# Forget attention of a two-block transformer on one core: heads transposed and scored in pairs, forget sums added as a broadcast row

## The chip, the cores and the metric

The kernel runs on one core of a Trainium2 chip, in float32 throughout. The metric is the device time of one execution in microseconds (us).

## What is computed

The reference is a chain of two transformer blocks on 512 tokens of 1024 features: a first block (gated delta rule, spatial gating, mixture of experts), and a second block with two layers, each an attention followed by a mixture of experts. The change is in the attention of the second block's first layer, the "forget attention" (`fox` in the names). It has 16 heads of 64 features:

```
proj = h @ w_in                                # 1024 -> 3 * 1024 + 16
q, k = rmsnorm(q, q_norm), rmsnorm(k, k_norm)  # per head, 64 features
log_f = log_sigmoid(f_logit + b_f)             # one number per token and head
cum = cumsum(log_f, over tokens)
s = q @ k.T * 64 ** -0.5 + cum[query] - cum[key]
p = softmax(where(key <= query, s, -inf))
o = (p @ v) @ w_out
```

`cum[query]` is one constant for a row of the softmax and cancels in it, so only `-cum[key]` has to be added to the scores. The attention of the second layer (`mla`, 96 features a head, no forget term) uses the same function of the kernel and is not changed.

## The kernel before

The kernel is a sequence of stages. A stage is a block in which each engine has its own list of instructions; all engines meet at its end. Within a stage they wait for each other by step numbers: `PE.done(ins, name)` counts a step of TensorE, `PE.wait(engine, name)` lets another engine wait for it (AC is ScalarE, DV VectorE, PO GpSimd, sp SyncE, the engine that only issues DMAs). Every engine works strictly in the order of its list. Tokens are in 4 blocks of 128 (T = 4, P = 128), and weights stream through a ring of four buffers in chunks of up to 2 MB, which `W.issue(sp)` loads on SyncE's queue as soon as the buffer's last reader is done.

**The projection stage** (L2331 to L2539) makes q, k and v in 24 jobs of 16 matmul passes with 512 columns. Beside them it makes the forget numbers: `forget` at job 8, `running_sums` at job 12, and ScalarE's copy of the negated sums (L2465). These go into the 65th column of every key head (`qkv_f[1][..., FD]`), while GpSimd writes 1.0 into the 65th column of every query head (L2533). A contraction over 65 features then gives score minus the key's sum, with no further instruction. VectorE also reduces 48 slabs of another weight matrix (`ada`) that are loaded by SyncE throughout the stage; the last thing that SyncE does in the stage is to issue the second 2 MB chunk of the output projection's weights (`fox_w_out`), whose buffer comes free with the last job.

**The attention stage** (`attention`, L2140 to L2308, called at L2541) walks over 64 units. A unit is a head and a block of 128 queries; block t needs (t + 1) x 128 keys. Units go by pairs of heads: (head 0, block 0), (head 1, block 0), (head 0, block 1), and so on, 8 units a pair. For each unit

- TensorE multiplies q and k (`S`, L2224) into one of three PSUM banks,
- VectorE adds the causal mask and takes the negated maximum in one instruction (`neg`, L2281), the mask being one tile for all heads, made once by GpSimd (L2300, L2302),
- ScalarE takes the exponential and its sum (`exp`, L2253), VectorE the reciprocal (`inv`, L2289),
- GpSimd multiplies by it (`share`, L2307),
- TensorE transposes the shares (`turn`, L2214), four units after their scores,
- ScalarE, or for the widest block VectorE, copies them out of PSUM (`pT`, L2263, L2296),
- and after both heads' units TensorE multiplies with v (`pv`, L2234). The two heads of a pair write to the lower and the upper 64 partitions of one bank, so each uses half of the array's columns.

q and k lie as tokens x features and are transposed by TensorE one head at a time (`turn_head`, L2191), 4 transposes each for q and for k, two pairs ahead in a ring of four heads, with copies by ScalarE (L2242) and VectorE (L2269). SyncE has nothing to do in this stage.

## Time and profile before

| | us |
|---|---|
| median of 3 runs | 2099.71 (2099.28 to 2102.07) |
| the profiled execution, its own time | 2096.7 |
| its span in the profile | 2095.0 |
| the projection stage | about 1049 to 1233.5 |
| the forget attention | about 1235.0 to 1329.5 |
| the other attention, for comparison | about 1715 to 1812 |

```text
span 2095.0 us, 20480 instructions
## 1 busy us (share of the span) xinstructions
PE 2017.3 (96%) x7494; PEld 1087.0 (52%) x7494; DVE 977.2 (47%) x1817; ACT 451.0 (22%) x1094; POOL 337.5 (16%) x474
## 2 busy tenths in 40 slices
PE   8999999999999999999899999999998999999994
PEld 4444444579884444444445457554444557544442
DVE  2444535557773024333454656343344467444333
ACT  1112111023342001100241136220004446320000
POOL 1000000000102000334200013103331003203333
PEclk9999999999999999999999999999999999999997
DMA  5223365610012234599816850047995120046996
GB/s 183 90 101 130 109 249 186 215 66 2 1 50 92 79 102 160 219 405 400 301 62 216 312 192 2 14 168 304 403 391 183 63 103 2 3 161 226 372 375 243
DMA packets 123511, 363.32 MB, mean 173 GB/s; under 512 B 27596, under 2 KB 33000, under 8 KB 110864
## 3 DMA queue, kind: packets, MB, share of 16 engines
q1 hardware_dynamic: 77856, 174.13, 23.4%
q10 hardware_dynamic: 30432, 157.30, 19.2%
q0 software_dynamic: 15120, 30.53, 4.2%
q8 instruction: 63, 1.03, 0.2%
q14 instruction: 40, 0.33, 0.0%
HBM read 335.60 MB, written 43.52 MB: 181 GB/s over the span
## 5 line engine op out<-in xcount | busy, mean ns | idle before, releaser
L1617 PE MATMUL bank<-ring,work 128*128 128x512 f32 x768 | 342.5, 599 | 3.3 <-DVE work L1633 3.3
L1617 PEld LDWEIGHTS bank<-ring,work 128*128 128x128 f32 x768 | 144.1, 193 | 167.8 <-issue 167.8
L1916 POOL DMA_INDIRECT work<-x_rows,small x168 | 169.1, 1007 | 269.5 <-DVE work L1881 197.4
L1628 PE MATMUL bank<-ring_halves,work 128*128 128x512 f32 x384 | 172.9, 593 | 4.0 <-DVE work L1642 4.0
L432 PE MATMUL bank<-featT,ring 128*128 128x512 f32 x384 | 170.3, 597 | 2.8 <-DMA ring<-in_w_in 2.8
L2404 PE MATMUL bank<-ring,featT 128*128 128x512 f32 x384 | 168.9, 601 | 1.6 <-DVE small L2493 1.6
L1345 PE MATMUL bank<-ring,work 128*128 128x512 f32 x384 | 166.5, 593 | 3.5 <-PEq L2186 2.4
L1639 DVE TENSOR_TENSOR work<-work,bank 128x256 f32<-128x256 f32 x48 | 20.2, 420 | 282.4 <-ACT work L1636 282.4
L2404 PEld LDWEIGHTS bank<-ring,featT 128*128 128x128 f32 x384 | 73.7, 193 | 93.8 <-issue 92.0
L1628 PEld LDWEIGHTS bank<-ring_halves,work 128*128 128x128 f32 x384 | 72.8, 190 | 95.0 <-issue 95.0
L1345 PEld LDWEIGHTS bank<-ring,work 128*128 128x128 f32 x384 | 72.3, 190 | 91.6 <-issue 91.6
L432 PEld LDWEIGHTS bank<-featT,ring 128*128 128x128 f32 x384 | 71.8, 192 | 84.7 <-issue 81.7
L531 PE MATMUL bank<-ring,featT 128*128 128x512 f32 x256 | 110.4, 593 | 0.9 <-PEq L412 0.9
L1636 ACT ACTIVATE work<-bank 128x256 f32<-128x256 f32 x48 | 18.4, 383 | 414.9 <-PE bank L1617 414.9
L2224 PE MATMUL bank<-work 65*128 65x384 f32 (+7 forms) x256 | 89.2, 434 | 0.5 <-DVE work L2269 0.5
L2307 POOL TENSOR_SCALAR ring_halves<-ring_halves,small 128x128 f32<-128x128 f32 (+3 forms) x128 | 67.7, 532 | 115.4 <-DVE small L2289 115.4
L1881 DVE STREAM_TRANSPOSE work<-work 128x1024 f32<-128x1024 f32 x42 | 85.0, 2024 | 0.0
L1062 PE MATMUL bank<-ring,featT 128*128 128x512 f32 x192 | 83.3, 593 | 1.0 <-PEq L811 1.0
L531 PEld LDWEIGHTS bank<-ring,featT 128*128 128x128 f32 x256 | 48.5, 190 | 61.4 <-issue 61.4
L2253 ACT ACTIVATE ring_halves<-bank,small 128x128 f32<-128x128 f32 (+3 forms) x128 | 67.5, 528 | 54.2 <-DVE small L2289 53.0
L286 DVE SCALAR_TENSOR_TENSOR ring_halves<-ring_halves,ismall 128x1024 f32<-128x1024 f32 x48 | 61.6, 1282 | 30.4 <-DMA ring_halves<-in_w_ada 26.8
L453 DVE TENSOR_SCALAR work<-bank,small 128x512 f32<-128x512 f32 x24 | 18.0, 751 | 107.4 <-PE bank L432 107.4
(444 smaller groups left out, 2826.7 us busy)
## 6 DMA issues: line engine op xcount, KB each, us to landing
ring<-in_w_in SPq DMA_DIRECT2D x15, 2048.0 KB, 12.5
ring<-in_moe_w_gate ACTq DMA_DIRECT2D x28, 1024.0 KB, 6.9
ring<-in_moe_w_up ACTq DMA_DIRECT2D x28, 1024.0 KB, 9.9
ring_halves<-in_moe_w_down ACTq DMA_DIRECT2D x28, 1024.0 KB, 10.2
ring_halves<-in_w_ada SPq DMA_DIRECT2D x48, 512.0 KB, 6.4
y_rows<-work ACTq DMA_DIRECT2D x48, 512.0 KB, 10.3
ring<-in_expert_w_gate ACTq DMA_DIRECT2D x14, 1024.0 KB, 7.9
ring<-in_expert_w_up ACTq DMA_DIRECT2D x14, 1024.0 KB, 10.9
```

The lines of the kernel that those rows point to most:

```text
L432: last = nc.tensor.matmul(bank[b % 4][:, :], w[:, k, (b % 4) * P:(b % 4 + 1) * P], featT[:, k, :], start=(k == 0), stop=(k == KD - 1))
L531: last = nc.tensor.matmul(uv_bank(j)[:, :], featT[:, k, t * P:(t + 1) * P], w[:, k, :], start=(k == 0), stop=(k == KD - 1))
L1062: last = nc.tensor.matmul(zg_bank(j)[:, :], featT[:, k, t * P:(t + 1) * P], w[:, k, :], start=(k == 0), stop=(k == KD - 1))
L1345: last = nc.tensor.matmul(bank[j % 4][:, :], outT[:, k, t * P:(t + 1) * P], w[:, k, :], start=(k == 0), stop=(k == KD - 1))
L1617: last = nc.tensor.matmul(gu_sum[par], xgT[par][:, k, :], w_gu[par][:, k, :, :], start=(k == 0), stop=(k == KD - 1))
L1628: last = nc.tensor.matmul(bank[5 + h][:, :], hT[par][:, k, :], w_dn[par][:, k, span(h)], start=(k == 0), stop=(k == KF - 1))
L1881: nc.vector.transpose(xgT[par].rearrange("p k (s b) -> p s k b", s=NQ), xg[par].rearrange("p (s a k) -> p s k a", s=NQ, k=KD)).then_inc(M_ ...
L1916: nc.gpsimd.indirect_dma_start(out=xg[par][:, s * QD:(s + 1) * QD], out_offset=None, in_=x_quarters, in_offset=bass.IndirectOffsetOnAxis(a ...
L2224: PE.done(nc.tensor.matmul(bank[i % N_S][:, 0:(t + 1) * P], qT[:, t * P:(t + 1) * P], kT[:, 0:(t + 1) * P], start=True, stop=True), ("S", i))
L2253: AC.done(nc.scalar.activation(sx[i % N_SX][:, 0:n], bank[i % N_S][:, 0:n], ACT.Exp, bias=mx[:, i:i + 1], scale=-1.0, accum_out=inv[:, i:i ...
L2307: PO.done(nc.gpsimd.tensor_scalar(x, x, inv[:, i:i + 1], 1.0, ALU.mult, ALU.mult), ("share", i))
L2404: last = nc.tensor.matmul(f_bank(j)[:, :], featT[:, k, t * P:(t + 1) * P], w[:, k, :], start=(k == 0), stop=(k == KD - 1))
```

## The change

It has four parts, all for the forget attention.

1. The 65th columns go. q and k have 64 features a head and are stored without a gap; the memset of ones falls away on GpSimd and VectorE.
2. The negated running sums (16 numbers a token) are transposed by TensorE at job 14 (`sums_by_row`), copied by ScalarE, and stored to DRAM by GpSimd's queue (`key_rows`, 16 heads x 512 keys). From there each head's row is loaded into all 128 partitions, once for each query block t with (t + 1) x 128 keys: 4 DMAs and 655 KB a head. Heads 0 and 1 are loaded on GpSimd's queue in the projection stage, heads 2 to 15 by SyncE in the attention stage, into four buffers in turn; head h >= 4 waits until VectorE has made the last `neg` of head h - 4. GpSimd then writes the causal mask into the diagonal 128 x 128 part of each tile with an `affine_select`, 4 for each head. VectorE's instruction adds this tile where it added the common mask.
3. q and k are transposed for two heads at once (`turn_pair`): 128 columns in, one head's features on the lower 64 partitions and the other's on the upper 64. The two heads' scores are then matmuls with a contraction over 64, one on each half of the array's rows.
4. The stage has a function of its own, `fox_attention`, with 32 steps of two units. A step's order on TensorE is q or k transposes of the next pair, `pv` of four steps back, both heads' `S`, both heads' `turn` of two steps back. Reciprocals are taken for two units at once; VectorE copies the upper head's transposed shares, ScalarE the lower head's and the output; scores have four banks and shares eight buffers.

```diff
         FD = DM // NHB
-        FW = FD + 1
-        QKV = T * NHB * FW
-        qkv_f = [work[:, i * QKV:i * QKV + T * NHB * n].rearrange("p (t h n) -> p t h n", t=T, h=NHB) for i, n in enumerate((FW, FW, FD))]
-        FOX_END = 2 * QKV + T * DM
+        qkv_f = [work[:, i * T * DM:(i + 1) * T * DM].rearrange("p (t h n) -> p t h n", t=T, h=NHB) for i in range(3)]
+        FOX_END = 3 * T * DM
...
-        gains = small[0:FD, 256:258]
+        gains = small[0:2 * FD, 256:258]
...
+        f_rows = work[0:NHB, F0 + 928:F0 + 928 + S]
+        key_rows = nc.dram_tensor("key_rows", [NHB, S], F32, kind="Internal").ap()
+        rows_stored, bias_landed, first_bias_landed = sem("key_rows_stored"), [sem(f"bias_landed{i}") for i in range(4)], [sem(f"first_bias_landed{i}") for i in range(2)]
+        B0 = FOX_END + 2 * 2 * S
+        SEG = [P * (t + 1) for t in range(T)]
+        bias_at = [[work[:, B0 + o:B0 + o + n] for o, n in zip((0, 128, 384, 768), SEG)],
+                   [work[:, o:o + n] for o, n in zip((F0, B0 + 1280, F0 + 128, B0 + 1536), SEG)],
+                   [work[:, F0 + 512 + o:F0 + 512 + o + n] for o, n in zip((0, 128, 384, 768), SEG)],
+                   [a[:, o:o + n] for a, o, n in zip((state, work, state, state), (0, F0 + 1792, 128, 512), SEG)]]
+
+        def load_bias(eng, h):
+            for t in range(T):
+                eng.dma_start(bias_at[h % 4][t], key_rows[h:h + 1, 0:SEG[t]].partition_broadcast(P)).then_inc(first_bias_landed[h] if h < 2 else bias_landed[h % 4], 16)
...
-        F_AT, CUM_AT, Q_AT, K_AT = 8, 12, 9, 17
+        F_AT, CUM_AT, ROWS_AT, Q_AT, K_AT = 8, 12, 14, 9, 17
...
+
+                def sums_by_row():
+                    AC.wait(pe, "cum")
+                    for t in range(T):
+                        last = nc.tensor.transpose(bank[0][0:NHB, t * P:(t + 1) * P], f_cum[:, t * NHB:(t + 1) * NHB], ident[:, :])
+                    PE.done(last, "cum_rows")
...
-                        AC.done(nc.scalar.activation(qkv_f[1][:, :, :, FD], T4(bank[0][:, NR:2 * NR], NHB), ACT.Copy, scale=-1.0), "cum")
+                        AC.done(nc.scalar.activation(f_cum, bank[0][:, NR:2 * NR], ACT.Copy, scale=-1.0), "cum")
+                    if j == ROWS_AT:
+                        PE.wait(act, "cum_rows")
+                        AC.done(nc.scalar.activation(f_rows, bank[0][0:NHB, :], ACT.Copy), "cum_rows")
                     if j in (Q_AT, K_AT):
                         i = 0 if j == Q_AT else 1
                         DV.wait(act, ("eps", i))
...
-                PE.wait(pool, ("sum",) + jobs[7])
-                PO.done(nc.gpsimd.memset(qkv_f[0][:, :, :, FD], 1.0), "ones_q")
+                AC.wait(pool, "cum_rows")
+                pool.dma_start(key_rows[:, :], f_rows).then_inc(rows_stored, 16)
+                pool.wait_ge(rows_stored, 16)
+                for h in range(2):
+                    load_bias(pool, h)
...
-        oT2 = attention(FW, *qkv_f, FOX_END, FOX_END + 2 * TURNED_HEADS * S, None, k_gain)
+        def fox_attention(q, k, v, turned_at, out_at):
...
+            sx = [halves_of_ring[:, i * BANK:(i + 1) * BANK] for i in range(8)]
...
+            NP = NHB // 2
+            both = range(2)
+            steps = [(p, t) for p in range(NP) for t in range(T)]
+            N = len(steps)
+            TURN_LAG, PV_LAG = 2, 4
+            END = N + PV_LAG
+            q_at = {T * (p - 1): p for p in range(1, NP)}
+            k_at = {T * (p - 1) + 2: p for p in range(1, NP)}
+            out_at_step = {T * p + T - 1 + PV_LAG: p for p in range(NP)}
+            select_at = {**{T * p - 1: 2 * p + 2 for p in range(1, NP - 1)}, **{T * p: 2 * p + 3 for p in range(NP - 1)}}
+            turn_bank, out_bank, X = (bank[4], bank[5]), bank[6], bank[7]
...
+            with nc.Block() as block:
+                @block.sync
+                def _(sp):
+                    for h in range(2, NHB):
+                        if h >= 4:
+                            DV.wait(sp, ("neg", 2 * (T * ((h - 4) // 2) + T - 1) + h % 2))
+                        load_bias(sp, h)
+                @block.tensor
+                def _(pe):
+                    def turn_pair(b, x, p, name):
+                        for t in range(T):
+                            last = nc.tensor.transpose(b[:, t * P:(t + 1) * P], x[:, t, 2 * p:2 * p + 2, :].rearrange("p h n -> p (h n)"), ident[:, :])
+                        PE.done(last, name)
+                    turn_pair(X, q, 0, ("q", 0))
+                    turn_pair(out_bank, k, 0, ("k", 0))
+                    for j in range(END):
+                        if j in q_at:
...
+                            turn_pair(X, q, q_at[j], ("q", q_at[j]))
+                        if j in k_at:
+                            AC.wait(pe, ("q", k_at[j]))
+                            turn_pair(X, k, k_at[j], ("k", k_at[j]))
+                        if j >= PV_LAG:
+                            i = j - PV_LAG
+                            p, t = steps[i]
+                            AC.wait(pe, ("pT", 2 * i))
+                            DV.wait(pe, ("pT", 2 * i + 1))
+                            if t == 0 and p:
+                                AC.wait(pe, ("out", p - 1))
+                            for s in range(t + 1):
+                                for m in both:
+                                    last = nc.tensor.matmul(out_bank[FD * m:FD * (m + 1), t * P:(t + 1) * P], v[:, s, 2 * p + m, :], pT[(2 * i + m) % len(pT)][:, s, :],
+                                                            start=(s == 0), stop=(s == t))
+                            PE.done(last, ("pv", i))
+                        if j < N:
+                            p, t = steps[j]
...
+                            if j >= 2:
+                                AC.wait(pe, ("exp", 2 * (j - 2) + 1))
+                            qT, kT = turned[p % 2]
+                            for m in both:
+                                PE.done(nc.tensor.matmul(bank[(2 * j + m) % 4][:, 0:(t + 1) * P], qT[FD * m:FD * (m + 1), t * P:(t + 1) * P], kT[FD * m:FD * (m + 1), 0:(t + 1) * P],
+                                                         start=True, stop=True), ("S", 2 * j + m))
+                        if TURN_LAG <= j < N + TURN_LAG:
+                            i = j - TURN_LAG
+                            for m in both:
+                                PO.wait(pe, ("share", 2 * i + m))
+                                if i:
+                                    (DV if m else AC).wait(pe, ("pT", 2 * (i - 1) + m))
+                                for s in range(steps[i][1] + 1):
+                                    last = nc.tensor.transpose(turn_bank[m][:, s * P:(s + 1) * P], sx[(2 * i + m) % len(sx)][:, s * P:(s + 1) * P], ident[:, :])
+                                PE.done(last, ("turn", 2 * i + m))
...
+                @block.scalar
...
+                    for j in range(END):
+                        if j in out_at_step:
+                            p = out_at_step[j]
+                            PE.wait(act, ("pv", T * p + T - 1))
+                            AC.done(nc.scalar.activation(outT[:, p, :], out_bank[:, :], ACT.Copy), ("out", p))
+                        if j < N:
+                            n = (steps[j][1] + 1) * P
+                            for m in both:
+                                i = 2 * j + m
+                                DV.wait(act, ("neg", i))
+                                if i >= len(sx):
+                                    PE.wait(act, ("turn", i - len(sx)))
+                                AC.done(nc.scalar.activation(sx[i % len(sx)][:, 0:n], bank[i % 4][:, 0:n], ACT.Exp, bias=mx[:, i:i + 1], scale=-1.0, accum_out=inv[:, i:i + 1]), ("exp", i))
...
+                        if TURN_LAG <= j < N + TURN_LAG:
+                            to, turned_x = keep_turned(act, 0, j - TURN_LAG)
+                            AC.done(nc.scalar.activation(to, turned_x, ACT.Copy), ("pT", 2 * (j - TURN_LAG)))
...
+                @block.vector
...
+                    for j in range(END):
+                        if j < N:
+                            p, t = steps[j]
+                            for m in both:
+                                i = 2 * j + m
+                                scores = bank[i % 4][:, 0:(t + 1) * P]
+                                PO.wait(dve, ("bias", 2 * p + m, t))
+                                PE.wait(dve, ("S", i))
+                                DV.done(nc.vector.tensor_tensor_reduce(scores, scores, bias_at[(2 * p + m) % 4][t], -1.0, 3.0e38, ALU.add, ALU.min, mx[:, i:i + 1]), ("neg", i))
+                        if TURN_LAG <= j < N + TURN_LAG:
+                            to, turned_x = keep_turned(dve, 1, j - TURN_LAG)
+                            DV.done(nc.vector.tensor_copy(to, turned_x), ("pT", 2 * (j - TURN_LAG) + 1))
+                        if j in k_at:
+                            keep_k(X, k_at[j])
+                        if j < N:
+                            AC.wait(dve, ("exp", 2 * j + 1))
+                            DV.done(nc.vector.reciprocal(inv[:, 2 * j:2 * j + 2], inv[:, 2 * j:2 * j + 2]), ("inv", j))
...
+                @block.gpsimd
+                def _(pool):
+                    def select(h, t):
+                        d = bias_at[h % 4][t][:, t * P:(t + 1) * P]
+                        if h < 2:
+                            pool.wait_ge(first_bias_landed[h], 16 * T)
+                        else:
+                            pool.wait_ge(bias_landed[h % 4], 16 * T * ((h - 2) // 4 + 1))
+                        PO.done(nc.gpsimd.affine_select(out=d, in_=d, compare_op=ALU.is_ge, fill=-3.0e38, base=0, pattern=[[-1, P]], channel_multiplier=1), ("bias", h, t))
+                    for h in range(3):
+                        for t in range(T):
+                            select(h, t)
+                    for j in range(N):
+                        for m in both:
+                            for i in both if j in select_at else ():
+                                select(select_at[j], 2 * m + i)
+                            x = sx[(2 * j + m) % len(sx)][:, 0:(steps[j][1] + 1) * P]
+                            DV.wait(pool, ("inv", j))
+                            PO.done(nc.gpsimd.tensor_scalar(x, x, inv[:, 2 * j + m:2 * j + m + 1], 1.0, ALU.mult, ALU.mult), ("share", 2 * j + m))
+            return outT
...
+        oT2 = fox_attention(*qkv_f, FOX_END, F0 - KD * S)
```

## Rows read from the trace of the kernel before

**Rows 1.** The page's busy line of TensorE: us, share, instructions.
```profile
PE 2017.3 (96%) x7494; PEld 1087.0 (52%) x7494; DVE 977.2 (47%) x1817; ACT 451.0 (22%) x1094; POOL 337.5 (16%) x474
```

**Rows 2.** Busy time of each engine in the steady part of the forget attention.
```profile
core 0: us, PE busy (x) PEld busy (x) DVE busy (x) ACT busy (x) POOL busy (x), PEclk, DMA share, GB/s
...
1240.00:1325.00 85.00, 85.00 (x656) 58.89 (x654) 57.71 (x217) 55.52 (x181) 32.10 (x61) 1.00 0.02 7
```

**Rows 3.** The first transpose of shares, in order of time.
```profile
1240.12 0.27 PE L2214 MATMUL bank<-ident,ring_halves 128*128 128x128 f32 x1
```

**Rows 4.** TensorE in order of time: start us, us, instructions (one pair).
```profile
1267.61 0.44 PE L2234 MATMUL bank<-featT,work 128*64 128x128 f32 x4
...
1275.48 1.10 PE L2234 MATMUL bank<-featT,work 128*64 128x128 f32 x16
1276.50 0.65 PE L2191 MATMUL bank<-ident,work 128*65 128x128 f32 x4
...
1277.21 1.02 PE L2224 MATMUL bank<-work 65*128 65x512 f32 x2
1278.07 0.38 PE L2214 MATMUL bank<-ident,ring_halves 128*128 128x128 f32 x2
1278.29 1.02 PE L2224 MATMUL bank<-work 65*128 65x512 f32 x2
1279.24 0.44 PE L2234 MATMUL bank<-featT,work 128*64 128x128 f32 x4
1279.61 0.65 PE L2191 MATMUL bank<-ident,work 128*65 128x128 f32 x4
1280.10 0.49 PE L2214 MATMUL bank<-ident,ring_halves 128*128 128x128 f32 x3
```

**Rows 5.** VectorE in order of time, one 512-key score block.
```profile
1278.27 0.70 DVE L2281 CUSTOM_DVE_ANT_0 bank<-bank,featT 128x512 f32<-128x512 f32 x1 [0.33 <-PE bank L2224]
1278.88 0.14 DVE L2281 DVE_READ_ACCUMULATOR2_ANT small<- 128x1 f32 x1
```

**Rows 6.** GpSimd's groups with shapes apart: busy us, mean ns.
```profile
L2307 POOL TENSOR_SCALAR ring_halves<-ring_halves,small 128x512 f32<-128x512 f32 x32 | 22.1, 692 | 20.4 <-DVE small L2289 20.4
...
L2307 POOL TENSOR_SCALAR ring_halves<-ring_halves,small 128x128 f32<-128x128 f32 x32 | 11.9, 372 | 24.8 <-DVE small L2289 24.8
...
L2302 POOL TENSOR_SCALAR_AFFINE_SELECT featT<-featT 128x128 f32<-128x128 f32 x2 | 0.6, 292 | 0.3 <-POOL featT L2300 0.2
```

**Rows 7.** SyncE's DMA issues in order of time, before the attention.
```profile
1207.60 0.33 SPq L262 DMA_DIRECT2D ring_halves<-in_w_ada  x1
1207.97 0.43 SPq L120 DMA_DIRECT2D ring<-in_fox_w_out  x1
...
1228.11 0.33 SPq L266 DMA_DIRECT2D ada_part<-ring_halves  x1
1234.10 0.38 SPq L120 DMA_DIRECT2D ring<-in_fox_w_out  x1
```

**Rows 8.** DMA issues of the whole run: KB each, us to landing.
```profile
ring<-in_moe_w_gate SPq DMA_DIRECT2D x4, 1024.0 KB, 4.8
...
x_rows<-work SPq DMA_DIRECT2D x8, 512.0 KB, 2.6
```

**Rows 9.** DMA from 1233 to 1250 us in 40 slices, and its issue.
```profile
GB/s 0 0 0 0 0 72 270 222 405 371 395 357 357 405 429 400 400 434 328 92 0 0 0 0 0 0 0 0 0 0 0 39 0 0 0 0 0 0 0 0
...
ring<-in_fox_w_out SPq DMA_DIRECT2D x1, 2048.0 KB, 7.8
```

**Rows 10.** TensorE in order of time after two pauses.
```profile
1027.10 5.39 PE L2024 MATMUL bank<-work,ones 128*128 128x512 f32 x12 [2.41 <-PEq L1324]
...
1046.17 1.94 PE L2049 MATMUL bank<-ident,work 128*128 128x128 f32 x8 [4.98 <-ACT work L2076]
```

**Rows 11.** Granted clock (PEclk) behind these two pauses.
```profile
1027.00:1031.00 4.00, 3.90 (x9) 1.82 (x10) 0.00 (x0) 3.92 (x5) 1.72 (x2) 1.00 0.48 136
1046.10:1049.40 3.30, 3.23 (x10) 2.10 (x10) 2.25 (x5) 1.50 (x4) 0.00 (x0) 0.50 0.00 0
```

More of the change, by code:

```diff
@@ L2366, in _ @@
             def _(sp):
-                load(sp, gains[:, 0:1], D["fox_q_norm_2"].rearrange("o p -> p o"))
-                load(sp, gains[:, 1:2], D["fox_k_norm_2"].rearrange("o p -> p o"))
+                for m in range(2):
+                    load(sp, gains[FD * m:FD * (m + 1), 0:1], D["fox_q_norm_2"].rearrange("o p -> p o"))
+                    load(sp, gains[FD * m:FD * (m + 1), 1:2], D["fox_k_norm_2"].rearrange("o p -> p o"))
                 cb_a.all_stored(sp)
```

65 lines of the change are left out of this document (57 added, 8 removed).

## Prediction

> **What bounds the kernel now.** I read the page's busy line first: TensorE is busy for 96% of the span [rows 1], so a change pays by what it takes from TensorE's path, and costs what it makes TensorE wait. Then the windows by stage: in 85 us of steady forget attention TensorE is busy for all 85, while VectorE and ScalarE are busy for 58 and 56, GpSimd for 32, and the DMA engines for 2% [rows 2]. The reader is to see an engine with no holes and three with slack. The timeline of TensorE gives the prices: a pair of heads takes 1279.24 - 1267.61 = 11.63 us [rows 4], and eight of them 93.0 us.
>
> The sum is made against the profiled execution's own time, 2096.7 us (span 2095.0 and 1.7 around it); the median of the runs shown is 2099.7, 3.0 above it, and I add that at the end. A measurement of this kernel can tell about 0.2%, 4.2 us, from no change.
>
> **Prices of TensorE.** Starts of successive groups [rows 4]: two 512-column passes take 0.86 us, so 128 columns take 0.107; two transposes take 0.22, also 0.11 each; the group of four head transposes takes 0.49. A `pv` group with 16 passes takes 1.02 us, where one after the other would be 1.71: its two column halves run beside each other. The group of 4 takes 0.37. Both fit (passes / 2 + 1) x 0.107 + 0.05: the halves overlap except for one pass, since each head makes two passes in a row, and 0.05 goes at the change of the array's shape. Entering `pv` costs another 0.09 to 0.10 (1278.29 + 0.86 = 1279.15 against 1279.24).
>
> **Part by part: a pair after the change, without waits.** Head transposes: 2 groups in place of 4, 0.97. Transposes of shares: 20, as before, 2.2. `pv`, as before: 2.77 for its four groups (0.37, 0.59, 0.80, 1.02; the middle two by the formula), and 0.40 to enter. Scores: per block of t + 1 key blocks four passes, which stood one behind the other (4.27 a pair). The row halves are not in the trace; the nearest row is `pv`'s column halves, so I take the same one-pass stagger, three passes of four, 3.21, and 4 x 0.08 for the third change of shape in each step. Bounds: two passes (2.14, full overlap) and four (4.27, none). Sum 0.97 + 2.2 + 2.77 + 0.40 + 3.21 + 0.32 = 9.87, 1.75 less than before. Other engines: VectorE loses one head copy and one reciprocal in two, ScalarE gains the output copy and loses a head copy; with 27 us of slack in 85 [rows 2] neither is the bound. Adding a bias tile costs VectorE nothing, as the mask was already read there [rows 5].
>
> **The loads of heads 4 to 15.** Here a wait takes the place of what is won. At step 3 of a pair (t = 3) VectorE ends the `neg` that frees head 4's buffer; call that moment 0. SyncE then issues four DMAs at a pitch of 0.37 us [rows 7], so the last starts at 1.1 and carries 262 KB. Its landing: a store of 512 KB lands after 2.6 us and a load of 1024 KB after 4.8 [rows 8]; at the 0.4 MB/us of [rows 9] the smaller size takes off 0.6 and 2.0, which leaves 2.0 to 2.8, and I take 2.5, nearer the load. So head 4 is there at 3.6 (3.1 to 3.9).
>
> GpSimd's list at that same step is: two `select` of head 4, share(6), two `select`, share(7). A share that is ready at about 2 us stands behind a mask for a head whose scores come five steps later. Four selects of 0.29 and two shares of 0.69 [rows 6] are 2.55; gaps between GpSimd instructions I take as 0.08 (0 to 0.15, the idle time before a select [rows 6]), 3.05 in all. TensorE needs share(6) and share(7) two steps later, for turn(3) in step 5, and everything is queued behind it there. Wanted at about 2.06 + 1.48 = 3.5 us (step 4, then `pv` and `S` of step 5), share(7) comes at 3.6 + 3.05 = 6.65.
>
> The loop closes: from there to the next such `neg` TensorE has turn(7) 0.43, head transposes 0.48, `pv` 0.90, `S` 1.04, a turn 0.22, `pv` 1.12, and the first 512-key score with its `neg`, 1.81 (score at 1277.21 to VectorE's last read at 1279.02 [rows 4, 5]): 6.00. With 0.1 for the hand-over a period is 3.6 + 3.05 + 0.1 + 6.0 = 12.75 us against 11.63: +1.12. This happens for heads 4, 6, ..., 14, six times. The odd head's loads and selects follow one step later, when GpSimd is already late, so they add nothing. Six bound pairs: +6.7. Two free ones: -3.5.
>
> **The start of the stage.** GpSimd's list begins with 12 selects, of which four wait for head 2; then, before share(0), two of head 3. Both heads are loaded by SyncE, whose last issue of the stage before is 2 MB of `fox_w_out` at 1234.10 [rows 7]. It lands at 1241.9, its bytes moving until about 1241.3 at 0.4 MB/us [rows 9]. Heads 2 and 3 stand behind it in the same queue: 1.31 MB more, 3.3 us, and 0.6 to the semaphore: 1245.2. Two selects (0.74) and share(0) (0.45), two more and share(1): 1247.6. TensorE reached its first turn at 1240.12 [rows 3] and would be there at about 1240.3 now (one more score pair, fewer head transposes). It waits 7.3 us.
>
> The Trainium skill ("DMA: Bandwidth & Descriptors", queue model) says that each DMA engine consumes a queue's descriptors in ring order. By it the landing is at 1245.2 as above; no row shows two such loads side by side.
>
> The pause has a second price. After a pause of 4.98 us [rows 10] the granted clock was 0.50, the lower level of 1.2 GHz, for 3.3 us; after one of 2.41 us it was 1.00, 2.4 GHz [rows 10, 11]. 3.3 us at half clock lose 1.65. Start: +8.95.
>
> **The rest.** Four transposes at job 14 stand on TensorE's path: +0.5. The 1.31 MB for heads 0 and 1 share the DMA engines with the slabs, 3.3 us of them; the last slab's store was issued at 1228.11 and the stage's last issue is at 1234.10 [rows 7], which with 2.6 us to land [rows 8] leaves 3.4 us, so nothing; without that cover up to 1 us. Selects of heads 0 and 1 (3 us) end before anything waits for them. The dropped memsets were off the path. Sum: 6.7 - 3.5 + 8.95 + 0.5 = +12.7: own time 2109.4, median **2112.4**.
>
> **Rivals.** (1) *Loads hidden, no slower than before.* If head 4's load landed before GpSimd came to it, the selects would fill its idle time and cost TensorE some 0.3 a pair: 8 x (10.2 - 11.63) = -11.4, with start and transposes -2.0: 2097.7. Place: share(6), share(7) of each pair. Price: 1 us of landing moves the whole by 6. The kernel breaks even at a period of 10.6, a landing 1.5 us after `neg`; four issues alone take 1.1 and no row lands in 0.4. Against it only that I may have misread who is queued behind whom. 12%.
> (2) *Row halves fully beside each other.* Scores take two passes: -1.07 in each free pair, -0.32 in each bound one (only t = 2 lies on the loop), -4.0 in all: 2108.4. For it, the two heads write different banks and partitions; against it the stagger of `pv`. 15%. The Trainium skill ("TensorE: Matmul & The Clock Gate", Part 3) has packed tiles start about 4 ns apart; this rule would give the two passes, though this case's `pv` rows show one pass more.
> (3) *No overlap of the halves*, so the change doesn't do what it says on TensorE: +4.0, 2116.4. 6%.
> (4) *The pauses inside the pairs cost clock too.* They would be about 1.8 and 0.9 us with a turn between them, shorter than the 2.41 that cost nothing. If each cost what the long one did, 6 x 1.65 = +9.9: 2122.3. A slower landing ends in the same place. 12%.
> (5) My forecast, 55%.
>
> If heads 2 and 3 don't queue behind the 2 MB, they land near 1241, the pause is 3.1 and keeps the clock: 5.8 less, a bound of the forecast and not a rival.
>
> **Numbers.** Bounds of the forecast: landing and gaps +-2.7 each, score passes +-4.0, start -5.8 and +1.9 (if a short packet takes as long as a long one, 5.2 us for two heads in place of 3.3). Not all fall one way: 2104 to 2120. To leave out no more than 2 in 10 with rivals on both sides the range is 2099 to 2124. Faster by over 0.2%: 0.08 (half of rival 1 and some tail), within 0.2%: 0.10, slower: 0.82.
>
> **What would show it.** In the profile after: a hole of TensorE of 6 to 7 us from about 1240, ended by GpSimd's share, with a clock of 0.50 behind it; GpSimd waiting for DMA into `work` or `state` at heads 2 and 3, then every 12 to 13 us; two short holes before `turn` in six pairs; and free pairs of 9.9 us at the end. A `S` group of two heads at t = 3 in 1.3 us says three passes, 0.9 two, 1.7 four. The forecast is wrong if `turn` never waits for GpSimd, if the first hole is under 3 us, or if the pairs in between are shorter than 11.6 us.

## The result, and the profile after

| | median us | runs | of the kernel before beside it |
|---|---|---|---|
| before | 2100.51 (2099.28 to 2102.07) | 4 | |
| after | 2157.06 (2149.86 to 2160.53) | 4 | ratio 1.0264, 95% interval 1.0237 to 1.0292 |

The change costs 56.6 us. The forecast was a cost of 12.7 us, with a range that ended at 2124. The profiled execution of after has a time of 2160.53 us and a span of 2158.7, 63.7 above the span of before; it is the slowest of the four, which is why the stages below are compared one by one.

The page of after, its busy line:

```profile
PE 2021.8 (94%) x7434; PEld 1085.2 (50%) x7434; DVE 967.8 (45%) x1784; ACT 447.7 (21%) x1079; POOL 359.2 (17%) x544
```

TensorE's busy time has hardly moved from [rows 1], so what was added is mostly waiting; what some stretches cost more at a lower clock was saved in others. TensorE in order of time, from the start of the attention stage (L2616 transposes heads, L2651 makes scores, L2660 transposes shares, L2639 multiplies with v, L1345 is the stage behind):

```profile
1239.53 2.89 PE L2616 MATMUL bank<-ident,work 128*128 128x128 f32 x12 [4.29 <-PEq L2375]
...
1254.57 0.48 PE L2660 MATMUL bank<-ident,ring_halves 128*128 128x128 f32 x1 [8.00 <-POOL ring_halves L2737]
...
1269.12 2.29 PE L2660 MATMUL bank<-ident,ring_halves 128*128 128x128 f32 x8 [5.86 <-POOL ring_halves L2737]
...
1280.44 0.85 PE L2660 MATMUL bank<-ident,ring_halves 128*128 128x128 f32 x6 [0.98 <-ACT featT L2693]
...
1288.24 2.29 PE L2660 MATMUL bank<-ident,ring_halves 128*128 128x128 f32 x8 [5.73 <-POOL ring_halves L2737]
...
1389.25 6.25 PE L1345 MATMUL bank<-ring,work 128*128 128x512 f32 x14 [0.95 <-PEq L2604]
```

The reader is to see the hole at the start, and then, in six of the eight pairs, a hole of 5.3 to 6.0 us ahead of the transposes of shares, which in before was never there. Six of them stand 17.7 to 19.1 us apart (the first at 1269.12, the last at 1361.18: 92.06 us for five periods, 18.4 each), against 11.63 a pair in [rows 4]. From the first head transpose to the first matmul of the next stage the attention takes 149.7 us; in before it took 95.9 by the same marks. That is 53.9 of the 63.7 us. The projection stage took 3.7 more (from its first job at 1050.42 to 1239.53, against 1049.66 to 1235.03), and 6 us lie in stages that the change doesn't touch, of which nothing here says why. The medians, 56.6 us apart, are close to 53.9 + 3.7 without them.

The waits between 1239 and 1385 us (waited for: us in total, times, longest) say who holds whom:

```profile
POOL work L2727 <- DMA work<-key_rows: 64.4, 10, 9.6
...
PEld bank L2660 <- POOL ring_halves L2737: 54.0, 22, 8.6
...
PE bank L2660 <- POOL ring_halves L2737: 42.4, 8, 8.0
```

GpSimd's mask (L2727) waits for a load, and TensorE waits for GpSimd's multiplication (L2737) that stands behind the mask. One turn of this loop in order of time (L2709 is VectorE's `neg`, L2341 a load of a broadcast row):

```profile
1258.68 0.73 DVE L2709 CUSTOM_DVE_ANT_0 bank<-bank,work 128x512 f32<-128x512 f32 x1
1258.85 6.67 SPq L2341 DMA_DIRECT2D work<-key_rows  x8
...
1267.84 0.54 POOL L2727 TENSOR_SCALAR_AFFINE_SELECT work<-work 128x128 f32<-128x128 f32 x2 [9.62 <-DMA work<-key_rows]
1268.37 0.69 POOL L2737 TENSOR_SCALAR ring_halves<-ring_halves,small 128x512 f32<-128x512 f32 x1
1269.02 0.54 POOL L2727 TENSOR_SCALAR_AFFINE_SELECT work<-work 128x128 f32<-128x128 f32 x2
...
1269.55 0.69 POOL L2737 TENSOR_SCALAR ring_halves<-ring_halves,small 128x512 f32<-128x512 f32 x1
...
1278.56 1.74 SPq L2341 DMA_DIRECT2D work<-key_rows  x4
```

From the first issue (1258.85) to the mask (1267.84) 9.0 us; the masks and shares to 1270.24, 2.4; from there to the next first issue (1278.56) 8.3: 19.7 us. The forecast had 3.6, 3.05 and, with the hand-over, 6.1. The landing is the term that was most wrong. In the other five turns the time from the first issue to the mask is 8.0 to 8.7 us. The loads between 1256 and 1276 us (KB each, median us from issue to landing):

```profile
DMA packets 1154, 1.34 MB, mean 67 GB/s; under 512 B 128, under 2 KB 896, under 8 KB 1152
...
work<-key_rows SPq DMA_DIRECT2D x2, 256.0 KB, 7.0
...
work<-key_rows SPq DMA_DIRECT2D x2, 64.0 KB, 5.0
```

A load of 256 KB, which is what I reckoned with, takes longer than the 1024 KB load of [rows 8]. These medians mix the even head's piece with the odd head's; the even head alone is shown with e3 below. The two heads' 1.31 MB were there 12.8 us after the first issue, 103 GB/s, against 400 for the 2 MB of [rows 9]. (The 67 GB/s of the line above is a mean over the window, idle time included.) The windows (the number after the busy times is the granted clock) add the second price:

```profile
1240.00:1300.00 60.00, 36.92 (x233) 23.47 (x232) 21.19 (x80) 21.24 (x70) 18.96 (x53) 0.74 0.32 96
...
1269.00:1275.00 6.00, 5.82 (x28) 3.94 (x28) 0.76 (x2) 0.60 (x1) 3.91 (x12) 0.51 0.13 39
...
1288.00:1294.00 6.00, 5.70 (x36) 4.09 (x38) 1.28 (x5) 0.60 (x1) 4.03 (x12) 0.67 0.17 51
```

Behind each hole TensorE works at a granted clock of 0.50, the level of 1.2 GHz, for a while: close to 6 us behind three of the six, 3.1 to 4.0 behind the others. Eight transposes take 2.29 us there, and 1.09 where the clock is whole. In before the granted clock was 1.00 through the whole stage.

### The profile page after: what moved, and what is told of

The parts are those of the page before. It is cut to its first block and busy times, and to the rows that moved or that the text cites. A ratio compares the mean times of both kernels' runs of the same rounds, so it can differ in the third digit from the quotient of the medians.

```text
span 2158.7 us, 20555 instructions
## 1 busy us (share of the span) xinstructions
PE 2021.8 (94%) x7434; PEld 1085.2 (50%) x7434; DVE 967.8 (45%) x1784; ACT 447.7 (21%) x1079; POOL 359.2 (17%) x544
## 5 line engine op out<-in xcount | busy, mean ns | idle before, releaser
L1345 PE MATMUL bank<-ring,work 128*128 128x512 f32 x384 | 166.5, 593 | 3.0 <-PEq L2186 1.1
L2422 PEld LDWEIGHTS bank<-ring,featT 128*128 128x128 f32 x384 | 73.3, 192 | 93.0 <-issue 91.3
L1345 PEld LDWEIGHTS bank<-ring,work 128*128 128x128 f32 x384 | 72.2, 190 | 91.2 <-issue 91.2
L1636 ACT ACTIVATE work<-bank 128x256 f32<-128x256 f32 x48 | 18.4, 384 | 416.2 <-PE bank L1617 416.2
L2660 PE MATMUL bank<-ident,ring_halves 128*128 128x128 f32 x160 | 32.9, 342 | 51.0 <-POOL ring_halves L2737 42.4
L286 DVE SCALAR_TENSOR_TENSOR ring_halves<-ring_halves,ismall 128x1024 f32<-128x1024 f32 x48 | 61.5, 1282 | 41.8 <-DMA ring_halves<-in_w_ada 38.3
L531 PEld LDWEIGHTS bank<-ring,featT 128*128 128x128 f32 x256 | 48.5, 190 | 61.4 <-issue 61.4
L1062 PEld LDWEIGHTS bank<-ring,featT 128*128 128x128 f32 x192 | 36.1, 190 | 44.7 <-issue 44.7
L869 PE MATMUL bank<-work 128*128 128x128 f32 x384 | 57.4, 277 | 0.2
```

What stands on the lines that cost most here:

```text
L286: DV.done(nc.vector.scalar_tensor_tensor(out=acc, in0=w, scalar=c_cols[:, k:k + 1], in1=acc, op0=ALU.mult, op1=ALU.add), ("slab", i))
L531: last = nc.tensor.matmul(uv_bank(j)[:, :], featT[:, k, t * P:(t + 1) * P], w[:, k, :], start=(k == 0), stop=(k == KD - 1))
L869: unit(u, lambda o, h: nc.tensor.matmul(o, lev[:, h, :], inv_t[:, h, :], start=True, stop=True), ("dinv", l, u))
L1062: last = nc.tensor.matmul(zg_bank(j)[:, :], featT[:, k, t * P:(t + 1) * P], w[:, k, :], start=(k == 0), stop=(k == KD - 1))
L1345: last = nc.tensor.matmul(bank[j % 4][:, :], outT[:, k, t * P:(t + 1) * P], w[:, k, :], start=(k == 0), stop=(k == KD - 1))
L2422: last = nc.tensor.matmul(f_bank(j)[:, :], featT[:, k, t * P:(t + 1) * P], w[:, k, :], start=(k == 0), stop=(k == KD - 1))
```

## The experiments

"Stage" below is the attention stage between the marks given above (before 95.9, after 149.7 us), in one profiled execution each. e2, e3, e8 and e11 leave the forget sums out or add other numbers in their place, so they show times and not a kernel that could be used.

| | median us | ratio to before (95%) | stage | a pair in the middle |
|---|---|---|---|---|
| e1, masks late | 2115.82 | 1.0065 (1.0044 to 1.0085) | 104.7 | 11.8 |
| e2, no loads | 2092.19 | 0.9961 (0.9949 to 0.9973) | 90.3 | 10.43 |
| e3, own rows | 2130.99 | 1.0142 (1.0115 to 1.0169) | 126.1 | 13.5 to 17.3 |
| e4, packed | 2116.96 | 1.0085 (1.006 to 1.0111) | 114.1 | 12.9 to 14.7 |
| e5, packed and late | 2101.84 | 1.000 (0.999 to 1.001) | 95.6 | 10.43 |
| e6, first loads earlier | 2099.02 | 0.9991 (0.9982 to 1.0001) | 90.6 | 10.43 |
| e7, only first loads earlier | 2157.04 | 1.0268 (1.025 to 1.0286) | 144.8 | 17.8 to 19.5 |
| e8, packed, own rows | 2113.7, one run | | 116.2 | 13 to 14 |
| e9, copies first | 2097.56 | 0.998 (0.9972 to 0.9989) | 91.9 | 10.43 |
| e10, loads ahead of the weights | 2091.22 | 0.995 (0.9936 to 0.9965) | 89.7 | 10.43 |
| e11, no loads, copies first | 2095.24 | 0.9963 (0.9949 to 0.9977) | 89.7 | 10.43 |

### Who holds the shares (e1)

```diff
-select_at = {T*p - 1: 2*p + 2 ..., T*p: 2*p + 3 ...}     # and two selects ahead of each share
+select_at = {T*p - 2: 2*p ..., T*p - 1: 2*p + 1 ...}     # all four behind the unit's shares
```

> The loads stay; only GpSimd's masks move: a head's four selects stand behind the shares of the last step or two before its first scores, not in front of share(6) and share(8) five steps ahead. Theory A (a mask that waits for its load holds up the shares queued behind it): the 5 to 6 us hole of TensorE in each of six pairs goes, and with it the half clock; pairs take 10 to 13 us in place of 18 to 19, still bound by two heads' loads (12.9 us from neg to the odd head's mask in the changed kernel). The time falls by 35 to 45 us, to 2110 to 2122. Rival B (the pairwise stage is slow by itself, through changes of the array's shape and TensorE's waits for ScalarE's copies): the holes only move to another wait, and the time falls by less than 15 us.

The edit moves a head's masks three steps later and behind the shares. The loads were nearly as slow as in after (in the middle pairs an even head was there 7.9 to 8.5 us after its first issue), and yet 41 of the 57 us were gone, as expected: it is the place of the masks in GpSimd's list that turns a late load into a stopped TensorE. TensorE in order of time:

```profile
1274.04 0.85 PE L2659 MATMUL bank<-ident,ring_halves 128*128 128x128 f32 x6 [0.99 <-ACT featT L2692]
...
1277.42 1.07 PE L2659 MATMUL bank<-ident,ring_halves 128*128 128x128 f32 x8 [1.32 <-POOL ring_halves L2734]
```

Two short holes are left in a pair, and behind them the clock was whole (1.00 over the 63 us from 1277). The one of 1.32 is made by the edit itself: the odd head's first mask now comes behind the widest shares (e5 moves it back, and the hole is gone). The one of 0.99 ends with ScalarE's copy.

### What the pairs bring without loads (e2)

```diff
-pool.dma_start(key_rows, f_rows) ... load_bias(pool, h) ... load_bias(sp, h)
+nc.gpsimd.memset(bias_at[0][t], 0.0)          # one mask, read for every head
```

> Leaves out the forget sums in the attention: no row is stored or loaded, all heads use one set of four tiles with zeros and the causal mask. Head pairs, row halves and order are as in the changed kernel. It shows what the pairwise part alone is worth. Theory A: pairs of 9.5 to 10 us, no wait for GpSimd at the start, the stage begins at 1235 as before the change (if the loads of heads 0 and 1 were what made it 4.5 us late); 2084 to 2090, 10 to 16 us faster than the kernel before. Rival B: pairs of 11.6 us or more, 2100 or above.

This is the rest of the change by itself, and it makes the kernel faster by 0.4%, at the low end of what Theory A had; its pairs are longer than the 9.5 to 10 us expected. One pair of it, TensorE in order of time:

```profile
1268.76 0.84 PE L2652 MATMUL bank<-ident,ring_halves 128*128 128x128 f32 x6 [0.99 <-ACT featT L2685]
...
1270.76 1.09 PE L2652 MATMUL bank<-ident,ring_halves 128*128 128x128 f32 x8
...
1275.26 1.13 PE L2643 MATMUL bank<-work 64*128 64x512 f32 x4
1276.32 0.66 PE L2652 MATMUL bank<-ident,ring_halves 128*128 128x128 f32 x4
...
1279.19 0.85 PE L2652 MATMUL bank<-ident,ring_halves 128*128 128x128 f32 x6 [0.99 <-ACT featT L2685]
```

A pair takes 1279.19 - 1268.76 = 10.43 us, 9.44 of work and a wait of 0.99. The four 512-column passes of both heads' scores take 1276.32 - 1275.26 = 1.06 us. Two passes take 0.86 [rows 4], so the row halves run beside each other, with 0.2 left over for the group; three passes one behind the other would be 1.29. Rival 2 was right. The whole stage gained 5.5 us, not 8 x (11.63 - 10.43) = 9.6, since in its first and last units TensorE has waits for ScalarE of up to 1.84 us that before did not have, and works at half clock for some 3.3 us behind the last of them (0.50 from 1320.6 to 1323.9).

### What makes the landing long (e3, e4, e8)

e3 keeps the small pieces and lets each partition read a row of its own:

```diff
-eng.dma_start(bias_at[h % 4][t], key_rows[h:h+1, 0:SEG[t]].partition_broadcast(P))
+eng.dma_start(bias_at[h % 4][t], D["x"][0][0:P, 0:SEG[t]])        # for h >= 2
```

> As the changed kernel, but heads 2 to 15 load other numbers: each partition reads its own row of the input x, in pieces of the same sizes, instead of all 128 partitions reading one row of key_rows (so wrong sums are added). Theory C (many reads of one DRAM row are what makes a 64 KB piece land after 5.0 us and a head after 9): landings fall to about 3 to 4 us, the holes before the turns to under 2 us, the time to 2115 to 2125. Rival D (four small DMAs one after another with packets of 512 bytes to 2 KB): landings and time stay within 5 us of the changed kernel.

The widest and the narrowest of the four loads of one even head, by KB and us to landing, first in the changed kernel (issued from 1258.85 us), then in e3 (from 1253.12), and TensorE of e3:

```profile
work<-key_rows SPq DMA_DIRECT2D x1, 256.0 KB, 7.5
...
work<-key_rows SPq DMA_DIRECT2D x1, 64.0 KB, 3.4
```

```profile
work<-in_x SPq DMA_DIRECT2D x1, 256.0 KB, 3.4
...
work<-in_x SPq DMA_DIRECT2D x1, 64.0 KB, 1.9
```

```profile
1272.76 2.29 PE L2660 MATMUL bank<-ident,ring_halves 128*128 128x128 f32 x8 [2.26 <-POOL ring_halves L2737]
```

The last piece is issued 1.3 us after the first, so the whole head lands 4.7 us after its first issue in place of 8.9; over the six pairs it is 4.4 to 5.8 in place of 7.9 to 8.9. The holes shrink from 5.3 to 6.0 us to 1.8 to 3.2, with a second one of 0.4 to 0.5 behind four of the six. The number and sizes of the transfers are the same, so 3 to 4 us of the landing come from where the bytes are read: 128 rows of `x` in place of one row of 2 KB. Theory C has the direction, but the landing and the time (2131, expected 2115 to 2125) stayed above what it expected.

e4 keeps the shared row and makes the pieces large: the row lies in DRAM as the four blocks' prefixes one behind the other, and a head comes in one to three transfers with 1 to 5 KB a partition instead of four with 0.5 to 2 KB. It changes a third thing too: the four transfers of the change all begin at the row's first byte, so that the same bytes are read again by each, while here no byte is in two transfers.

```diff
+for t in range(T): pool.dma_start(key_rows[:, PACK_AT[t]:PACK_AT[t] + SEG[t]], f_rows[:, 0:SEG[t]])
-for t in range(T): eng.dma_start(bias_at[h % 4][t], ...)
+for dst, at in pieces[h % 4]: eng.dma_start(dst, key_rows[h:h+1, at:at + dst.shape[1]].partition_broadcast(P))
```

> As the changed kernel, but a head's row is stored four times in one DRAM row, in the order of the tiles, and a head is loaded by 1, 2 or 3 DMAs with pieces of 1 to 5 KB in place of 4 DMAs: the same bytes, all still one DRAM row for 128 partitions. Theory D (number and size of the pieces): the even head's load lands some 3 to 4 us earlier, the time falls by 15 to 30 us. Theory C (one row for all): the bytes still come from one row, the landing falls by at most 1 to 2 us and the time by less than 10.

Its packets and its issues between 1256 and 1276 us:

```profile
DMA packets 580, 1.35 MB, mean 68 GB/s; under 512 B 64, under 2 KB 192, under 8 KB 576
...
work<-key_rows SPq DMA_DIRECT2D x1, 640.0 KB, 4.0
state<-key_rows SPq DMA_DIRECT2D x2, 256.0 KB, 4.1
work<-key_rows SPq DMA_DIRECT2D x1, 128.0 KB, 4.0
```

A whole even head lands 4.0 us after its issue, and the time fell by 40 us, more than either theory had. So the DRAM tensor, the same as in the change, is not slow for itself. The odd head of this window still comes from its one row in pieces of 2, 1 and 2 KB, and they too land after 3.9 to 4.4 us. So it is not the size of a piece alone either that made the landing long; the number of transfers, or that they all read the same 2 KB, may be part of it, and no run separates them. With 4.0 in place of 3.6 the forecast's loop is 4.0 + 3.05 + 0.1 + 6.0 = 13.15 us. Transposes ended such a wait at 1255.73, 1268.75, 1283.41, 1297.38 and 1310.30: 13.0, 14.7, 14.0 and 12.9. The loop holds where the clock is whole; the longer periods have a half-clock stretch in them:

```profile
1256.00:1268.00 12.00, 9.46 (x84) 6.00 (x82) 6.92 (x27) 6.97 (x23) 5.16 (x14) 1.00 0.33 106
1270.50:1273.80 3.30, 3.30 (x21) 2.19 (x19) 0.76 (x2) 0.00 (x0) 2.00 (x6) 0.50 0.03 5
1284.50:1287.00 2.50, 2.41 (x14) 2.09 (x16) 0.76 (x2) 0.20 (x1) 2.16 (x8) 0.50 0.00 0
```

e8 is e4 with rows of their own for heads 2 to 15, to see whether sharing costs large pieces anything:

```diff
-key_rows[h:h+1, at:at + dst.shape[1]].partition_broadcast(P)
+D["w_in"][0][0:P, at:at + dst.shape[1]]                            # for h >= 2
```

> Packed loads, but for heads 2 to 15 each partition reads its own row of another input (wrong sums are added). Theory C2 (one DRAM row for all partitions is slow only in small pieces): a head of 640 KB lands after 3.5 to 4.2 us as with one row for all, 4.0. Rival C (the shared row costs by itself): it lands after 3 us or less, and pairs shrink by 1 us or more.

640 KB landed in 4.4 us, no sooner than from one row, so in this form of the load the shared row costs nothing. What is slow is the shared row together with the four small transfers that start at the same byte: each of the two edits takes most of the delay away, and both together take no more.

### Both remedies together, and the start (e5, e6, e7)

e5 is e4 with late masks as in e1, but the odd head's first mask ahead of the last shares, which is to remove the hole of 1.32:

```diff
+if j in odd_at: select(odd_at[j], 0)
 for m in both: share(2 * j + m)
+if j in odd_at: select(odd_at[j], 1..3)
+if j in even_at: select(even_at[j], 0..3)
```

> Packed loads and late masks together; of the odd head's masks the first stands ahead of the pair's last shares, since with late masks alone VectorE waited for it (1.3 us a pair). Theory A: both repairs work on the same hole, so they don't add up. Pairs are no longer bound by loads and take 10.4 us as without any load, the hole at the start (head 2's load behind 2 MB) stays at about 4 us and the stage starts in time: 2094 to 2102. Rival B: pairs stay at 11.5 us or more, since GpSimd's and VectorE's order with masks costs more than the loads: 2105 or above.

The pairs are at 10.43 us, the same as with no loads at all, so in steady state the loads now cost nothing. The stage takes 95.6 us, as before the change; what is left is the start, a pause of 3.66 us and half clock behind it, where heads 2 and 3 land behind the 2 MB of weights:

```profile
ring<-in_fox_w_out SPq DMA_DIRECT2D x1, 2048.0 KB, 7.9
work<-key_rows SPq DMA_DIRECT2D x1, 640.0 KB, 8.6
```

8.6 us for what lands in 4.0 in the pairs. e6 issues these two heads in the projection stage (e7 does the same to after and changes nothing else):

```diff
 move_slabs(sp, beside, spread(SLABS, 6))
+sp.wait_ge(rows_stored, 16 * T)
+load_bias(sp, 2); load_bias(sp, 3)
 W.issue(sp)
```

> As packed loads with late masks, and heads 2 and 3 are loaded by SyncE at the end of the projection stage, ahead of the last 2 MB of weights. Theory: head 2 lands by the start of the attention, the pause before the first turn goes (no half clock behind it either), 4 to 6 us less than packed with late masks alone: 2089 to 2097, faster than the kernel before by 0.2 to 0.6%. Rival: the weights, now 1.3 MB later in the queue, or the issues before the stage's end, hold the stage up as much: no difference.

> The changed kernel with only the loads of heads 2 and 3 moved ahead of the last 2 MB (small pieces, masks as in the change). Theory: the first hole of 8 us falls to 3 us or less, and with it some half clock: 5 to 9 us less than the changed kernel, 2148 to 2152; the six pairs stay at 18 to 19 us. Rival: small pieces are slow with or without the 2 MB before them, the hole stays above 5 us and the time within 3 us of the changed kernel.

Both expectations missed: e6 came out within 0.2% of before and e7 no faster than after. The edit did not do what I took it to do. `move_slabs` itself issues the last 2 MB, so the loads were still behind them, and the stage's end had to wait for SyncE. e6 at SyncE, then TensorE of e6 and of e7:

```profile
1233.67 0.38 SPq L120 DMA_DIRECT2D ring<-in_fox_w_out  x1
1234.16 0.51 SPq L2346 DMA_DIRECT2D work<-key_rows  x1
```

```profile
1236.61 2.89 PE L2626 MATMUL bank<-ident,work 128*128 128x128 f32 x12 [2.97 <-PEq L2380]
```

```profile
1243.32 2.89 PE L2619 MATMUL bank<-ident,work 128*128 128x128 f32 x12 [10.04 <-PEq L2375]
...
1252.90 0.47 PE L2663 MATMUL bank<-ident,ring_halves 128*128 128x128 f32 x1 [1.34 <-POOL ring_halves L2740]
```

In e7 the pause of 8.00 us of the changed kernel shrank to 1.34, and the wait at the end of the projection stage grew from 4.29 to 10.04: it only moved to the other side of the mark.

### The last 0.99 us, and the loads really ahead (e9, e10, e11)

e9 is e6 with ScalarE's copy made a step later and, as I took it, ahead of its exponentials; e11 is e2 with the same edit:

```diff
-exp(j); if TURN_LAG <= j: copy(j - TURN_LAG)
+if TURN_LAG + 1 <= j: copy(j - TURN_LAG - 1); exp(j)
```

> The kernel of e6 (packed rows, masks added just before use, heads 2 and 3 loaded before the stage), and ScalarE makes its copy of each pair of turned shares one turn later, ahead of its exponentials instead of behind them. In e5 and e6 each pair took 10.43 us, of which 0.98 was TensorE waiting for ScalarE's copy. Theory A, that this wait is a matter of ScalarE's order alone: pairs of 9.6 us or less, some 6 us less than e6, about 2093 us and faster than before. Rival, that ScalarE is then late with the exponentials, so that the wait moves to the transposes of the shares: pairs stay at 10.4, 2099 us, within 0.2% of before.

> The kernel of e2 (no forget sums: nothing is loaded, and VectorE adds one mask for all heads) with ScalarE's copies ahead of its exponentials as in e9. It shows what working by pairs brings where nothing waits for a load. Theory A (the wait of 0.99 us in each pair is ScalarE's order alone): about 6 us less than e2, 2086 us. Rival (the exponentials come late instead): 2092 as e2.

Theory A's gain came in neither, but the edit did not test it. A copy that goes a step later and then ahead of that step's exponentials stands where it stood: behind the exponentials of the step before and ahead of this step's. All that changed in ScalarE's list is that in one step of four the output copy goes ahead of the copy of shares instead of behind it. ScalarE of e2 and of e9 at the same place (the copy of 128 columns is that of the shares, the one of 512 the output):

```profile
1275.86 0.28 ACT L2685 ACTIVATE featT<-bank 128x128 f32<-128x128 f32 x1
1276.02 0.61 ACT L2672 ACTIVATE work<-bank 128x512 f32<-128x512 f32 x1
```

```profile
1279.12 0.59 ACT L2690 ACTIVATE work<-bank 128x512 f32<-128x512 f32 x1
1279.59 0.28 ACT L2693 ACTIVATE featT<-bank 128x128 f32<-128x128 f32 x1
```

The wait split into two, 0.38 behind the exchanged copy and 0.56, and a pair still takes 10.43 (e9, TensorE):

```profile
1280.02 0.63 PE L2670 MATMUL bank<-ident,ring_halves 128*128 128x128 f32 x4 [0.38 <-ACT featT L2693]
...
1282.44 0.84 PE L2670 MATMUL bank<-ident,ring_halves 128*128 128x128 f32 x6 [0.56 <-ACT featT L2693]
```

So whether ScalarE's order is what holds a pair at 10.43 us stays open. What the traces do show is the way to that wait: from the widest scores (1275.26 in e2) over VectorE's `neg`, ScalarE's two exponentials of 0.69 us and the copy behind them to the transposes at 1279.19 are 3.93 us, and TensorE has 2.94 of work of its own in between (3.93 less the wait of 0.99). In e9 the same way takes 3.93 again. A copy truly ahead of these two exponentials was not tried.

e10 is e9 with the two heads' loads ahead of the last weights:

```diff
 for j in ...:                       # move_slabs
+    if j == issue_after[-1]: ahead_of_last()      # wait for the rows, load_bias(sp, 2), load_bias(sp, 3)
     for _ in range(issue_after.count(j)): W.issue(sp, 1)
```

> e9, and the loads of heads 2 and 3 are issued ahead of the last 2 MB of weights of the projection stage instead of behind them. In e6 and e7 they were issued behind these, and the pause of the start moved to the barrier ahead of the stage (2.97 us there in e6 against 0.96). Theory A, that the 2 MB ahead of them in the queues is what made the first loads late: the wait at the barrier is back at about 1 us and there is no pause ahead of the first transposes; 2 to 4 us less than e9, about 2090. Rival, that the loads are slow for themselves while the stage's slabs move: the barrier or the pause stays at 2 to 3 us, and the time is that of e9.

SyncE and TensorE of e10:

```profile
1234.57 0.43 SPq L2348 DMA_DIRECT2D work<-key_rows  x1
...
1237.46 0.38 SPq L120 DMA_DIRECT2D ring<-in_fox_w_out  x1
```

```profile
1238.39 1.07 PE L2629 MATMUL bank<-ident,work 128*128 128x128 f32 x8 [0.96 <-PEq L2382]
```

The wait at the stage's end is back at 0.96 us, head 2 lands 5.2 us after its issue, no transpose of shares at the start waits for GpSimd, and the kernel is 0.5% faster than before, 10.3 us by the medians, as fast as those without any load, and 6.3 faster than e9 where 2 to 4 were expected. Of this the attention stage shows 95.9 - 89.7 = 6.2 us; the rest lies between runs and outside it.

## Why the prediction was wrong, step by step

**The sign and the loop were right.** The order that was forecast (load, mask, share, transposes of shares) is in the trace, and e1 shows that the place of the masks on GpSimd is what carries it to TensorE. e4 supports the arithmetic of the loop: 13.0 us measured where the clock is whole, 13.15 by its terms. That it is so near is in part luck: in the turn up to 1268.75 the load took 4.4 up to the mask, GpSimd 2.4 and not 3.05, TensorE's part 6.2 us.

**The step that failed is the landing, "head 4 is there at 3.6 (3.1 to 3.9)".** It was 9.0 in the turn shown and 8.0 to 9.0 in all six, 8.4 on average, 4.8 too much. I had sized it by bytes, from a store of 512 KB and a load of 1024 KB [rows 8], and I had put no price on 128 partitions reading one row in small pieces. e3 and e4 show that own rows would have given 4.4 to 5.8 us and fewer, larger pieces 3.8 to 4.4; e8 shows that the two don't add up. So some 3.3 of the 4.8 are this kind of load, and over 1 more stayed with own rows, where the last of the four transfers took 3.0 to 4.4 us and not the 2.5 of the forecast. The pitch of the issues [rows 7] played little part: from the first issue of a head to the last were 1.3 us, against 1.1. The bounds of the range came from the same rows, so it was too narrow for the same reason: a kind of transfer that was in no row was bounded only by rows of another kind.

**Rival 4, "the pauses inside the pairs cost clock too", came with it.** It had 12%. In the turn shown the TensorE part of the loop took 8.3 us in place of 6.1, with a clock of 0.51 behind the hole. With 5.4 more of landing, 2.2 of clock and 0.65 less on GpSimd (2.4 against 3.05) the forecast's period of 12.75 becomes 19.7, the 1258.85 to 1278.56 of the trace. e4, whose pauses ahead of the transposes (0.6 to 1.8 us and then 0.5) are of the length that the forecast had, shows this rival for itself: half clock for some 3.4 us behind three of its six. The turn above is the longest; over the whole the periods are 18.4, 5.65 above the forecast, and six of them make 34 of the 41.8 us between the stage's +53.9 and the forecast's +12.15 for it (6.7 - 3.5 + 8.95). Counted the other way, from the first transpose of shares on the stage took 134.7 us against 90.8, 43.9 more: the six holes are 34.0, the waits for ScalarE 8.2, half clock behind the six holes about 14.0 (half of the time that TensorE works at 0.50; 1.5 to 2.9 each), behind the pause of the start 3.2 and at the stage's end 1.7, and the work by pairs saves 8 x (11.63 - 9.44) = 17.5; together 43.6.

**The start was right in kind, and its pause near in size partly by luck.** The pause was forecast as 7.3 us and was 8.00. But the loads of heads 2 and 3 were slow here too, so that the first transpose of shares came 15.0 us after the stage's first instruction, where the forecast had 12.4; and TensorE reached it after 7.0 us where the forecast had 5.1, which hid 1.9 of this. Half clock had already begun in the wait at the stage's end: the eight score passes at 1242.41 took 1.65 us there and 0.96 in e6. Behind the pause it cost 3.2 us, not 1.65. Together the start cost some 13 us (9.9 + 3.2), forecast 8.95. The Trainium skill ("DMA: Bandwidth & Descriptors", section "Queues, rings and completion order") has each engine consume a queue's descriptors in ring order; e5 (640 KB in 8.6 us behind the 2 MB) and e10 (5.2 ahead of them) agree.

**Row halves (rival 2).** Two passes, as that rival had it, not three. A free pair of 9.87 us was nevertheless near the 10.43 of e2, by three errors that nearly cancel: the scores gained 1.07, the groups of scores and of transposes cost 0.64 more than their prices from [rows 4] (9.44 against 8.80), and TensorE waited 0.99 for ScalarE, which the forecast had at nothing ("neither is the bound").

**The projection stage, "so nothing".** It took 3.7 us more. VectorE's waits for slabs in `ring_halves` rose from 6.8 to 17.3 us. Where heads 0 and 1 come in small shared pieces the stage took 189.1 to 190.9 us (after, e1, e3), in the others but e7, where SyncE's loads lengthen it, 184.1 to 187.9. In single profiled executions it varies by 2 us, so a cost of 2 to 4 is what can be said.

## What to carry to other kernels

Before you size a transfer by its bytes, look whether any row of the trace has its kind: size and number of the pieces, and whether the partitions share a source. If none has, the upper bound is open, and a loop that holds TensorE multiplies it. A load that is slow hurts only through the list it is waited for in: put the instruction that waits for it behind everything that does not need it, and issue it ahead of large transfers that can come later. And check in the trace where an issue really went; "before the stage ends" was not "before the weights". The same goes for an order of instructions: write out the engine's list before and after an edit; "a step later and ahead" left the copy where it was.

## What the hardware showed that was not expected

- One row of DRAM of 2 KB, read by all 128 partitions in four transfers with 0.5 to 2 KB a partition: the 640 KB of an even head were there 7.9 to 8.9 us after the first issue. From rows of their own, in the same four transfers, 4.4 to 5.8. From one row of 5 KB in one transfer 3.8 to 4.4, and in one transfer from own rows 4.1 to 4.5. Small pieces are not slow for themselves: the odd heads of e4 come from their one row in pieces of 1 to 3 KB, which land after 3.9 to 5.0 us.
- The granted clock after a pause does not follow from its length alone. After 2.41 us in before it was 1.00 [rows 10, 11], and after 2.02 us in e8 1.00 as well; after 2.26 us in e3 it was 0.50, and in e4, after 1.77 and after 1.84 us, it fell to 0.50 within 1.7 us of the pause. Those in e3, e4 and e8 came after other pauses of the same loop. Pauses of 0.99 and 1.32 us in each pair of e1 left it at 1.00.
- Float32 scores on the two row halves of the array run beside each other: four 512-column passes in 1.06 us, where two take 0.86 [rows 4].
